# A transformer pair on one core: modulation sums earlier, retention scores head by head, one more square root in the head loop

## The reference

```python
mod = adaln_params(c, w_mod, b_mod)            # silu(c) @ w_mod + b_mod, six rows of 1024
mod_c = adaln_params(c_ctx, w_mod, b_mod)
h = modulate(x, norm1_g, mod[0], mod[1])       # rms_norm(x) * g * (1 + scale) + shift
hc = modulate(ctx, norm1_g, mod_c[0], mod_c[1])
rq, rk, rv, rg, dq, dk, dv = split(h @ w_in)   # the same for hc: 7 parts, 3072 columns
# retention, 4 heads, dk 64, dv 128: scores = q k^T * decay (both directions), out = scores v,
#   rms_norm per head, times silu(rg)
# differential attention, 4 heads of 2 x 64: softmax(q1 k1) - lam * softmax(q2 k2), times v,
#   rms_norm per head; keys and values of the context come first
x = x + mod[2] * (concat(ret, diff) @ w_out)
h2 = modulate(x, norm2_g, mod[3], mod[4])
x = x + mod[5] * peer_ffn(h2)                  # 8 heads x 16 gathered experts per token
# second block: MoBA attention and gated delta rule, w_out, mixture of 32 experts, final norm
```

## Time and profile before

| | |
|---|---|
| median of 3 runs | 1347.79 us (1343.67 to 1347.83) |
| the profiled execution | 1347.79 us, its span 1346.0 us |
| busy share of the span | PE 85%, PEld 52%, DVE 56%, ACT 29%, POOL 21% |
| chain that ended last | PE 51%, DMA 34%, DVE 8%, ACT 4%, issue 2% |
| mean granted TensorE clock | 0.979 |

### The profile page before, as it was taken

The page is one execution under the profiler, slowest core; times in us unless marked ns, Lnnn a source line. Parts: engine busy times, 40 slices in busy tenths (PEclk is TensorE's granted clock), DMA queues, the critical chain, the costliest instruction groups (busy, mean ns, idle before and its releaser), DMA issues.

```text
span 1346.0 us, 16073 instructions
## 1 busy us (share of the span) xinstructions
PE 1149.4 (85%) x5796; PEld 705.1 (52%) x5796; DVE 758.2 (56%) x1958; ACT 388.1 (29%) x1087; POOL 288.6 (21%) x275
## 2 busy tenths in 40 slices
PE   6999999989999987787777777778999997877796
PEld 4887889845555532232232323226888885333342
DVE  1688764877677676777667776543842515311112
ACT  2203441342333332333332333223521423000011
POOL 0000000243434443444433444430030000000000
PEclk9999999999999999999999999999999988988999
DMA  9744344699999999999999999997421475999996
GB/s 393 302 167 152 113 176 186 258 419 346 423 421 421 421 421 421 422 420 422 422 416 416 416 422 406 418 409 318 156 76 52 188 297 221 426 426 423 425 388 253
DMA packets 60282, 446.77 MB, mean 332 GB/s; under 512 B 6704, under 2 KB 7088, under 8 KB 10160
## 3 DMA queue, kind: packets, MB, share of 16 engines
q0 software_dynamic: 36864, 268.45, 48.4%
q1 hardware_dynamic: 22912, 175.97, 32.3%
q10 hardware_dynamic: 432, 1.40, 0.3%
HBM read 444.74 MB, written 1.05 MB: 331 GB/s over the span
## 4 chain that ended last, share of the span: by engine, by line
PE 51%; DMA 34%; DVE 8%; ACT 4%; issue 2%; POOL 0%; SPq 0%; DVEq 0%; ACTq 0%; POOLq 0%
DMA arena<-uv_in,arena 25%; PE bank L2657 13%; PE bank L2502 7%; DMA wring<-moe_in 4%; PE bank L2763 4%; PE bank L3009 3%; PE bank L2618 3%; PE bank L3025 2%; DVE arena L1963 2%; PE bank L2566 2%; PE bank L2968 2%; DMA wring<-stream_in 2%; DMA arena<-moe_in 2%; PE bank L2760 2%; PE bank L2995 2%
## 5 line engine op out<-in xcount | busy, mean ns | idle before, releaser
L2657 PE MATMUL bank<-arena 128*128 128x512 f32 x1024 | 478.7, 611 | 118.7 <-ACT arena L1146 118.6
L1963 DVE CUSTOM_DVE_ANT_0 arena<-arena 128x1024 f32<-128x1024 f32 x256 | 313.5, 1225 | 192.4 <-DMA arena<-uv_in,arena 191.8
L865 POOL DMA_INDIRECT arena<-uv_in,arena x256 | 274.2, 1071 | 626.9 <-PE bank L2657 369.3
L2657 PEld LDWEIGHTS bank<-arena 128*128 128x128 f32 x1024 | 188.0, 192 | 378.1 <-ACT arena L1146 192.8
L1138 ACT ACTIVATE arena<-arena 128x2 f32<-128x2 f32 x128 | 26.2, 205 | 408.1 <-DVE arena L1963 407.9
L2502 PE MATMUL bank<-wring,arena 128*128 128x256 f32 x608 | 135.4, 383 | 1.5 <-DVE arena L1463 1.0
L2502 PEld LDWEIGHTS bank<-wring,arena 128*128 128x128 f32 x608 | 115.7, 192 | 18.8 <-DMA wring<-stream_in 1.4
L1146 ACT ACTIVATE arena<-const,arena 128x128 f32<-128x128 f32 x256 | 86.7, 386 | 0.0
L3009 PE MATMUL bank<-wring,arena 128*32 128x512 f32 x288 | 59.7, 620 | 7.8 <-DMA wring<-moe_in 7.8
L3009 PE MATMUL bank<-arena 128*32 128x512 f32 x288 | 59.7, 615 | 6.9 <-DMA arena<-moe_in 4.9
L1142 ACT ACTIVATE arena<-arena 128x1 f32<-128x1 f32 x256 | 61.4, 287 | 4.2
(11 more groups left out here) (490 smaller groups left out, 1372.1 us busy)
## 6 DMA issues: line engine op xcount, KB each, us to landing
wring<-stream_in SPq DMA_DIRECT2D x63, 1024.0 KB, 8.9
wring<-moe_in SPq DMA_DIRECT2D x14, 2048.0 KB, 17.8
arena<-moe_in SPq DMA_DIRECT2D x26, 1024.0 KB, 17.8
arena<-moe_in SPq DMA_DIRECT2D x12, 2048.0 KB, 18.5
wring<-moe_in SPq DMA_DIRECT2D x13, 1024.0 KB, 14.8
arena<-stream_in SPq DMA_DIRECT2D x4, 1024.0 KB, 8.3
arena<-uv_in,arena POOLq DMA_INDIRECT x256, 12.8
arena<-moe_in SPq DMA_DIRECT2D x4, 512.0 KB, 11.1
```

The lines of the kernel that those rows point to most:

```text
L865: pool.indirect_dma_start(G[:, j, :], None, uv_d, src).then_inc(gathered[j], 16)
L1963: v.tensor_tensor_reduce(out=junk, in0=G[:, j, 0:D], in1=h2[:, t, :], scale=1.0, scalar=0.0, op0=ALU.mult, op1=ALU.add, accum_out=dots[:, ...
L2657: ins = mm(bank[1 + 2 * tile + c][:, :], diag[:, j, :], G[:, j, D + c * 512:D + (c + 1) * 512], start=False, stop=False, skip_group_check= ...
```

## The change

Four things are moved or added. Two sums (m = 0 and 1) go ahead of VectorE's wait for the context's root; one (m = 2) stays where five were; the head loop carries m = 3 to 10, and m = 11 comes behind it, ahead of `diff_out(1)`; the table of SyncE follows. The norm of tile 0 of the differential attention moves from behind the masks to the end of the loop's last pass, and its root on ScalarE into pass 6. The other roots are merged, and a root of a constant is taken ahead of the retention's squares. The retention scores are formed head by head.

```diff
-SUMMED_EARLY = 5
-SUMMED_AFTER = {C_IN1 + 5: (0, 1), C_IN1 + 7: (2, 3, 4), C_IN1 + N_IN1 - 1: tuple(range(5, SUMMED))}
+SUMMED_AFTER = {C_IN1 + 5: (0, 1), C_IN1 + 7: (2, 3), C_IN1 + N_IN1 - 1: tuple(range(4, SUMMED))}
@@ ScalarE, loop over the parts
                 if p == 6:
                     diff_squares(0)
+                    head_roots(1, 0, 4)
             diff_squares(1)
-            head_roots(2, 0, 4)
-            head_roots(2, 8, 12)
+            nc.scalar.activation(lam2[:, 0:1], epsc, ACT.Sqrt)
             ret_squares(0)
-            head_roots(3, 4, 8)
+            head_roots(3, 4, 12)
@@ VectorE
+            dve.wait_ge(inputs_ready, 1)
+            mod_sum(0)
+            mod_sum(1)
+
             dve.wait_ge(rms_root, 2)
             link(v.reciprocal(rstd[:, 1], rstd[:, 1]))
@@
-            dve.wait_ge(inputs_ready, 1)
-            for m in range(SUMMED_EARLY):
-                mod_sum(m)
+            mod_sum(2)
             dve.wait_ge(proj_out, part_at(9, True) + 1)
@@ loop over the heads
-                if p + SUMMED_EARLY < SUMMED:
-                    mod_sum(p + SUMMED_EARLY)
+                if p == 7:
+                    norm_diff(0, 1)
+                mod_sum(p + 3)
+            mod_sum(SUMMED - 1)
             diff_out(1)
             mask_scores(0)
 ...
             mask_scores(3)
-            norm_diff(0, 1)
             modulation(3)
             modulation(4)
-            norm_ret(0, 3)
+            norm_ret(0, 2)
 ...
             norm_diff(1, 2)
-            norm_ret(1, 4)
+            norm_ret(1, 3)
@@ second block, the count of roots
-            dve.wait_ge(y_root, 5)
+            dve.wait_ge(y_root, 4)
@@ TensorE
-            def scores(a):
-
-                if a == 0:
+            def scores(h):
+                r = slice(RK * (h % 2), RK * (h % 2) + RK)
+                if h == 0:
                     pe.wait_ge(diff_exp, 2 * DH * NT)
-                else:
-                    pe.wait_ge(ret_masked, 2 * a)
+                if h >= 2:
+                    pe.wait_ge(ret_masked, h - 1)
                 for k in range(4):
-                    for h in (2 * a, 2 * a + 1):
-                        r = slice(RK * (h % 2), RK * (h % 2) + RK)
-                        ins = mm(bank[(4, 1)[h % 2] + k // 2][:, (k % 2) * T:(k % 2 + 1) * T],
-                                 rkT[r, h // 2, k * P:(k + 1) * P], rqT[r, h // 2, :], start=True, stop=True)
-                        if k == 3:
-                            ins.then_inc(ret_scores, 1)
+                    ins = mm(bank[(4, 1)[h % 2] + k // 2][:, (k % 2) * T:(k % 2 + 1) * T],
+                             rkT[r, h // 2, k * P:(k + 1) * P], rqT[r, h // 2, :], start=True, stop=True)
+                ins.then_inc(ret_scores, 1)
@@
             scores(0)
+            scores(1)
             pe.wait_ge(diff_aT_out, DH * NT)
+            outputs(0).then_inc(ret_y, 1)
+            scores(2)
+            outputs(1).then_inc(ret_y, 1)
+            scores(3)
             mod_turn(pe, 3)
-            outputs(0).then_inc(ret_y, 1)
-            scores(1)
-            outputs(1).then_inc(ret_y, 1)
             outputs(2, (0,))
             outputs(3, (0,)).then_inc(ret_y, 1)
```

## The result

| | before | after |
|---|---|---|
| median of 4 runs, same chip | 1347.24 us (1343.67 to 1347.83) | 1361.66 us (1358.52 to 1362.59) |
| ratio after to before, 95% interval | | 1.0108 [1.0084, 1.0133] |
| profiled execution | 1347.79, span 1346.0 | 1357.78, span 1355.9 |

The change costs 14.4 us by the medians. The forecast was 1358.1 with a range up to 1361.5: right in sign, 3.6 us too low, and the median lies just outside the range.

The account below looks back on a forecast made before the run. TensorE was taken as the chain from 47.9 to 106.6 us, then alternating with VectorE; the later gathers are DMA-bound. Terms 4.9 + 1.8 + 1.2 + 2.4 = 10.3 us on 1347.79 gave 1358.1, range 1352.5 to 1361.5.

Parts of the forecast that it names:

- rival C: Low clock lasts longer behind the context stall (+1.6) or returns behind head 7's wait (+1.8): 1360 to 1362; chance 0.10.
- Part 1: Sums 0 and 1 before the context's norm wait for their transfers: TensorE idles 4.9 us, then low clock loses 1.8.
- Part 2: Sums moved within the head loop: VectorE's lateness stays the same and later loads have cover; costed at nothing.
- Part 3: Square root at head 6: reloading the Exp table delays head 7, 1.2 us straight into TensorE's wait.
- Part 4: Retention scores by head lose the overlap of the two row halves: 2.4 us more up to turn 4.
- B: One softer term falls away: clock not lowered behind the stall (1356.3) or row halves still overlap (1355.8); chance 0.20.
- D: Chunks for sums 0 and 1 land in time, so no stall; only parts 3 and 4 count: 1351.4; chance 0.08.
- E: Not slower: VectorE's tail ended the retention stage, so moving tile 0's norm saves 1.8: 1346.8 or 1344.4; chance 0.07.

Follow-up runs that it names:

- e1: The changed kernel with sums 0 and 1 put back behind the context's norm; 1352.81 us, ratio 1.0056 to the kernel before.
- e5: The kernel before with only sums 0 and 1 moved ahead of the context's norm; 1352.71 us, ratio 1.0056.
- e7: The changed kernel with 11 matmuls, results unread, filling TensorE's wait for the first context chunk; 1355.70 us, ratio 1.0078 to the kernel before.
- e2: The changed kernel with tile 0's root on ScalarE moved behind head 7's exponentials and eviction; 1356.74 us, ratio 1.0086 to the kernel before.
- e8: The changed kernel with 6 matmuls, results unread, ahead of head 7's transposes on TensorE; 1359.80 us, ratio 1.0116 to the kernel before.
- e3: The changed kernel with paired scores and TensorE's old retention order restored; 1356.42 us, ratio 1.0075 to the kernel before.
- e13: The kernel before with scores head by head but turn 3 ahead of the first output and scores 2 and 3 in a row; 1348.35 us, ratio 1.0016.
- e11: The kernel before run once more, unchanged, a single execution; 1344.35 us.
- e10: The changed kernel run once more, unchanged, a single execution; 1359.22 us.
- e4: The changed kernel with early sums, root at head 7 and scores by head all undone; 1344.93 us, ratio 0.9990 to the kernel before.
- e12: The kernel before with only the change's head-by-head order of scores, a repeat as a single execution; 1350.91 us.
- e6: The kernel before with only the change's head-by-head order of scores; 1349.65 us, ratio 1.0033.

## Why the prediction was right in kind and too low in size

The forecast's sum and the measured one, both at the mark (216.33 before):

| term | forecast | measured in after | shown by |
|---|---|---|---|
| start of the projections | 0 | 0.3 | varies by execution |
| stall for the context's norm | 4.9 | 4.9 | e1, e5; its end is fixed |
| low clock behind it | 1.8 | 1.9 | e7 |
| Exp table at head 7 | 1.2 | 1.1 | e2 |
| low clock behind that wait | 0 (in rival C alone) | 1.5 | e2, e8; not in every execution (e7) |
| retention: scores by head | 2.4 | 2.8 | e2, e3, e13 |
| low clock in the retention | 0 | 1.5 | comes and goes, before too (e11) |
| sum | 10.3 | 14.0 | |

By the medians the change costs 14.4. The pair of e10 and e11 gives another sum: 15.2 us at the mark (231.41 against 216.20) and 14.9 in time. There TensorE was 1.3 us earlier at the context's norm, so that the stall is 6.3 and the low clock behind it costs 2.7; both have a late spell. So the cost lies between 14 and 15 us by execution, and the single base execution of the forecast, late at the start, made the stall look shorter than it often is. That the forecast missed the range by only 0.2 us says little: its terms were 3.7 us short at the mark.

**Part 1 was right.** The first sum started at 50.96 (forecast 50.7), the reciprocal at 58.79 (58.6), TensorE waited 4.90, and the clock fell behind it. Where the trace shows a transfer's issue and its landing, the start of a reader that is moved ahead can be read off. What I took for a constant, the 4.9, is a fixed end less TensorE's arrival: 4.4 to 6.5 us in six executions, all resumed between 63.35 and 63.46. That after gave exactly 4.90 is luck. In four of the six (e2, e3, e8, e10), with waits of 6.2 to 6.5, the clock fell during the wait, at 60.8 to 61.9, and stayed low 4.2 to 5.4 us behind its end, which costs 2.1 to 2.7 and not 1.8.

**Part 2 was right**: e3 and e4 show that the moved sums and the norm cost nothing.

**Part 3 was right as a wait.** VectorE's idle time grew by 1.22, and the load is 1.28: the load was all of the difference. The Trainium skill (ScalarE: Activation LUTs, What ACT_TABLE_LOAD costs) adds 1.38 us for a drain; as in the forecast, the trace doesn't show it: in after the root's load starts at 189.67, right behind the last square, its root at 190.97, and e2 gives back 1.24 us of wait, not 2.7.

**The step that failed** is a term that the sum put at nothing, the low clock behind head 7's wait. The forecast had it only in rival C: "the 2.4 us wait of head 7 lowers it again (+1.8; 2.45 us didn't elsewhere". It cost 1.5 to 1.7 us. From head 7's transposes to the first score it takes 9.35 to 9.40 us at the full clock (before, e2, e7, e8) and 10.85 to 11.05 where the clock fell (after, e1, e3, e10). Head 7's wait of 2.3 was followed by the low clock in four profiled executions of five (all but e7), its waits of 1.1 to 1.2 in none of eight. So on this evidence the wait is needed for it and does not bring it each time. One idle stretch of 2.45 us in the earlier trace rows was not enough to leave the term out, and the trace of before had others that speak against it. There is this wait of 2.24 us, for one, and the work behind it:

```profile
757.75:760.00 2.25, 0.01 (x2) 0.01 (x1) 2.16 (x8) 1.03 (x5) 1.68 (x1) 1.00 1.01 419
760.90:764.30 3.40, 3.40 (x5) 1.35 (x4) 3.15 (x12) 0.36 (x2) 1.10 (x1) 0.50 1.01 422
```

Of the eleven waits of 2.0 to 2.8 us that TensorE has at the full clock in that trace behind the first 250 us, five are followed by a fall within 1.3 us of their end. By that count about half of 1.6 us belonged into the sum (an estimate). The 1361.66 measured lies in rival C's 1360 to 1362, which had a chance of 0.10, but only the head 7 part of it is C's; as much again came from the late spell.

**Part 4** had the mechanism right. That its scores came out, 6.9 us forecast for four heads and 2.94 + 1.93 + 1.93 = 6.8 measured, is luck: one head takes 1.93 and not 1.73, and heads 0 and 1 in a row still overlap by 0.9 us, where the forecast had no overlap at all. The Trainium skill's rule that different tiles of the array can work in parallel (TensorEngine Tiling (Array Packing), Key Properties) agrees with e3 and e13; that the order in the list decides how much of it one gets is theirs. The 0.3 to 0.4 too little are heads 2 and 3, which stand apart and take 0.2 more each than the 1.73 of the sum; in e8, without a low clock, the rest comes as forecast, the turn at 1.81 (forecast 1.80) included.

**The low clock in the retention** stood in no case. It is not tied to this change: e11 has it in the kernel before. Counted over executions it adds 0 to 4.5 us ahead of the mark. Its cause stays open. What the forecast could have said is that its base was one execution: the profile of before showed no low clock from 48 to 233 us, and I took that for the kernel's.

**Rivals.** B is out for the clock: it was low behind the stall in six executions of six, and not with the wait filled (e7). Its other half, that "matmuls in the two halves might keep something at the border of two heads", came true for heads 0 and 1 (0.9 us). D is out (e5). E is out: with the norm moved and the scores in pairs, the retention takes the 12.12 and 17.80 us of before (e3), and with all three costly parts undone nothing measurable is gained (e4).

## What to carry to other kernels

Work put into an engine's idle time must have its data there, not only the engine free: read the landing of its transfer before moving it, and ask what is queued behind it. A forecast made of waits on TensorE should carry the low clock, by its share of cases, behind every wait as long as those that the trace sometimes shows it behind; one wait without it is no proof. And a profile is one execution: where it decides the base of a forecast, read a second one. For effects below 0.5%, compare stages between marks in two or three profiled executions; here the stages told apart 0.8 us while the medians could not tell 2.

## What the runs showed of the hardware

- TensorE's granted clock fell to 1.2 GHz without an idle stretch right ahead. In e12 it fell at 210.5 after 12.75 busy us of 13.2, for 10.3 us; in after at 221.0 after 7.50 of 7.50. In nine of 16 executions such a fall came in the retention, inside or just behind a turn. The cause was not found.
- Behind TensorE's waits of 4.4 to 6.5 us for the context the clock was low in six executions of six, behind waits of 2.3 at head 7 in four of five, behind waits of 1.1 to 1.2 there in none of eight. Where TensorE had work, 3.4 us at the low clock cost 1.3 to 1.7 us. Matmuls whose results nobody reads, put in place of the wait, kept the clock at the full level (e7, e8).
- Matmuls in the two halves of the rows, fp32 with 64 rows each, run beside each other fully when the program alternates them (16 records in 1.93 us), half when four of one half follow four of the other (16 records in 2.94), and not at all when they stand apart (8 records in 1.93). The engine did them in the order of its list, and that order decided how much ran in parallel (e3, e6, e13).
